# Products before a norm finished by halves of the rows, in a two-block float32 kernel

## The chip, the core and the metric

The kernel runs on one core of a Trainium2 chip. The metric is the device time of one execution in microseconds; the kernel before takes 1652.35 us (median of 3 runs, 1651.98 to 1653.06). A core has a matrix engine (TensorE, PE in the profile), a vector engine (VectorE, DVE), an activation engine (ScalarE, ACT), GpSimd (POOL) and a queue for transfers (SyncE, SP). Each works through its own list of instructions in order; semaphores connect them.

## The reference

Two transformer-like blocks, one after the other, on 512 rows (528 with 16 meta rows in the first block) of 1024 channels, in float32. What matters here is the shape that both have:

```python
h_res = h_res + rmsnorm(merged @ w_out, g_mix_post)          # out1, norm post1
h2 = rmsnorm(h_res, g_ffn_pre)                               # norm pre1f
up = centred_dwconv(h2 @ w_up, conv_w_ffn, conv_b_ffn)       # up1: 2 x 2816 channels
a, v = jnp.split(up, 2, axis=-1)
ffn_out = (jax.nn.gelu(a) * v) @ w_down                      # down1
h_res = h_res + rmsnorm(ffn_out, g_ffn_post)                 # norm post1f
```

`rmsnorm(x, g)` divides every row by the root of its mean square over the channels (plus 1e-6) and multiplies by the gain. The second block begins with another such norm (`pre2`) and a large product (first its gated part, `glu`, then the attention heads), and ends in the same way: `out2`, norm `post2`, norm `pre2f`, `up2`, `down2`, norm `post2f`.

## The kernel before

Channels lie on the 128 partitions, rows along the free dimension: the residual `res` is 8 channel blocks of 128 partitions by 528 rows. A product is made tile by tile, a tile being 128 output channels of all rows. The weights stream through four slots in pieces of 128 x 1024 numbers: SP loads a piece into `raw` as soon as the piece four before it is used (`w_used`), ScalarE writes its upper part (`w_to_hi`, L774) and VectorE the rest (`w_to_lo`, L1088). Operands are split in the same way, and a product is three passes (upper by upper, upper by rest, rest by upper; `three_passes`, L464). A one-piece tile is 8 channel steps k of three passes, in 512 columns or two times 258. A tile of `down` needs three pieces, 22 steps.

A norm of the output of a product goes as follows. ScalarE squares each finished tile (L782) and writes it, times the gain, into `mix1`, `mix2` or `down` (L939, L867, L1054); VectorE adds the squares up in `acc` (L1099). After the last tile TensorE sums over channels with a matmul by ones (`sum_channels`, L551), ScalarE takes the root (L788), VectorE inverts it (`inverse`, L1106 to L1110), and TensorE spreads the inverse over the partitions (`spread_inverse`, L562). `to_residual` (L1134) then does, for each of 8 blocks, a product (L1146 or L1148), an addition to `res` (L1150) and the rest part of the next operand (`cut_lo`, L1116), whose upper part ScalarE makes (L818 in `cut_residual`).

The norm in front of the next product isn't applied to its operand: the product begins on the unscaled residual, and each tile is scaled afterwards. So `norm_tiles` (L484) computes tiles 0 to 2 block by block as the operand appears, while ScalarE squares the residual and VectorE adds (`inverse_of_res`, L1129); then it sums the channels, and spreads the inverse in the middle of tile 3. ScalarE copies it into `rstd` (L798, L796), and from there on VectorE scales tile after tile, convolves, multiplies (`two_pairs`, per two pieces), and splits the weights in between, in a written order. ScalarE's order after the squares is: root, load of the table for the next function, upper part of piece 4, `rstd`, upper parts of pieces 5 and 6.

After `post2f` there is no next product: VectorE multiplies 8 blocks (L1620), GpSimd adds three of them to `res` (L451), VectorE five (L1623), and SP stores them.

## Time and profile before

| | us |
|---|---|
| median of 3 runs | 1652.35 |
| profiled execution, its own time | 1651.44 |
| its span, first to last instruction | 1649.6 |
| TensorE busy (matmuls) | 1590.9 |
| VectorE busy | 1108.0 |
| ScalarE busy | 549.6 |
| weight pieces, 272 of 512 KB | landing 3.5 each (median) |

The span counts from the first to the last instruction; the engines overlap, so their busy times don't add up to it. A busy time is a sum of instructions; consecutive matmuls overlap too, so a single one's duration is longer than its share, and the time of many divided by their number is what one costs.

### The profile page before, as it was taken

Reading aid. Unit: us, or ns where it says so; the run is one execution under the profiler, and the core shown is the slowest. Engines: PE = TensorE matmul, PEld = TensorE weight load, DVE = VectorE, ACT = ScalarE, POOL = GpSimd, SP = SyncE. Lnnn points to the kernel's source line nnn. Section 1 sums busy time; section 2 is a strip of 40 time slices with the busy share of each in tenths; the row PEclk is TensorE's granted clock in tenths of the full one; section 3 lists DMA queues with packets and bytes.
Section 4 is the critical chain, followed back from the end, with each engine's and each line's share of the span. In section 5 each row is a group of like instructions: output and inputs, shape, how many; then the busy total and the mean of one; then the engine's idle time right before and its main releaser. Section 6 shows DMA issues by size and latency. Waiting matters only on the chain.

```text
span 1649.6 us, 24134 instructions
## 1 busy us (share of the span) xinstructions
PE 1590.9 (96%) x9246; PEld 1408.3 (85%) x9246; DVE 1108.0 (67%) x1544; ACT 549.6 (33%) x742; POOL 34.3 (2%) x65
## 2 busy tenths in 40 slices
PE   8999999899999999989999999999998999999996
PEld 8999999899999988868887878877786788887885
DVE  5334456589888842277899998875556899887223
ACT  5123323342222232243333333556233322222231
POOL 1110000000000000000001001000000000000000
PEclk9999999899999999989999999999998999999998
DMA  4443212222323333323332222222322323332332
GB/s 168 122 122 96 93 52 90 64 90 90 89 89 91 96 95 114 102 70 93 98 90 83 77 84 84 80 75 82 97 90 63 100 92 102 91 100 89 113 104 76
DMA packets 43904, 152.51 MB, mean 92 GB/s; under 512 B 5850, under 2 KB 5862, under 8 KB 43840
## 3 DMA queue, kind: packets, MB, share of 16 engines
q1 hardware_dynamic: 41760, 147.26, 28.7%
q0 software_dynamic: 2080, 4.34, 1.1%
q8 instruction: 46, 0.75, 0.2%
q14 instruction: 18, 0.15, 0.0%
HBM read 149.44 MB, written 4.51 MB: 93 GB/s over the span
## 4 chain that ended last, share of the span: by engine, by line
PE 80%; DVE 14%; ACT 3%; DMA 1%; issue 1%; POOL 0%; DVEq 0%; SPq 0%; ACTq 0%
PE ps L464 77%; DVE work L1406 6%; DVE wlo L1088 2%; ACT whi L774 1%; DVE res L1150 1%; PE ps L562 1%; PE ps L651 1%; DVE tmp L1146 1%; PE ps L724 1%; DMA stats_dram<-head_stats 1%; DVE acc L1129 1%; ACT probs L973 0%; DMA raw<-w_dram 0%; DVE peaks L1450 0%; ACT L1019 0%
## 5 line engine op out<-in xcount | busy, mean ns | idle before, releaser
L464 PE MATMUL ps<-xh,whi 128*128 128x258 f32 (+2 forms) x2048 | 579.6, 331 | 16.2 <-DVE wlo L1088 8.9
L464 PE MATMUL ps<-xh,wlo 128*128 128x258 f32 (+2 forms) x2048 | 572.2, 328 | 0.0
L464 PE MATMUL ps<-xl,whi 128*128 128x258 f32 (+2 forms) x2048 | 571.8, 328 | 0.0
L1088 DVE TENSOR_TENSOR wlo<-raw,whi 128x1024 fp32r<-128x1024 f32 x272 | 331.9, 1220 | 167.2 <-ACT whi L774 166.6
L774 ACT ACTIVATE whi<-raw 128x1024 fp32r<-128x1024 f32 x272 | 287.0, 1058 | 438.4 <-DMA raw<-w_dram 438.2
L464 PEld LDWEIGHTS ps<-xh,whi 128*128 128x128 f32 x2048 | 347.8, 191 | 49.8 <-issue 17.2
L464 PEld LDWEIGHTS ps<-xh,wlo 128*128 128x128 f32 x2048 | 346.6, 190 | 33.8
L464 PEld LDWEIGHTS ps<-xl,whi 128*128 128x128 f32 x2048 | 347.2, 190 | 31.6 <-issue 0.5
L1406 DVE SCALAR_TENSOR_TENSOR work<-cin,vecs,work 128x512 f32<-128x512 f32 x240 | 180.2, 751 | 6.8
L464 PE MATMUL ps<-fh,whi 128*128 128x512 f32 x352 | 137.1, 390 | 2.3 <-DVE stage L1163 1.2
L464 PE MATMUL ps<-fl,whi 128*128 128x512 f32 x352 | 137.0, 389 | 0.0
L464 PE MATMUL ps<-fh,wlo 128*128 128x512 f32 x352 | 137.0, 389 | 0.0
L1099 DVE TENSOR_TENSOR acc<-acc,sq 128x512 f32<-128x512 f32 (+1 forms) x40 | 27.7, 693 | 121.4 <-ACT sq L782 121.3
L1163 DVE TENSOR_TENSOR stage<-ps,rstd 128x516 f32<-128x516 f32 x57 | 39.6, 695 | 68.1 <-PE ps L464 65.8
L464 PEld LDWEIGHTS ps<-fh,whi 128*128 128x128 f32 x352 | 66.1, 188 | 16.7 <-DVE stage L1158 1.6
L464 PEld LDWEIGHTS ps<-fl,whi 128*128 128x128 f32 x352 | 66.1, 188 | 13.7
L464 PEld LDWEIGHTS ps<-fh,wlo 128*128 128x128 f32 x352 | 66.1, 188 | 13.6
L1170 DVE SCALAR_TENSOR_TENSOR work<-stage,vecs,work 128x512 f32<-128x512 f32 x88 | 66.1, 752 | 10.6 <-DVE work L1167 1.5
L1167 DVE SCALAR_TENSOR_TENSOR work<-stage,vecs,work 128x512 f32<-128x512 f32 x88 | 66.2, 752 | 10.6 <-DVE work L1202 1.5
L782 ACT ACTIVATE sq<-ps 128x512 f32<-128x512 f32 (+1 forms) x32 | 19.2, 599 | 141.1 <-PE ps L464 141.1
L847 ACT ACTIVATE work<-work 128x512 f32<-128x512 f32 x44 | 27.8, 632 | 89.6 <-DVE work L1170 89.5
L464 PE MATMUL ps<-x2h,whi 128*128 128x512 f32 x128 | 51.0, 399 | 3.6 <-DVE x2l L1116 3.6
(201 smaller groups left out, 1510.9 us busy)
## 6 DMA issues: line engine op xcount, KB each, us to landing
raw<-w_dram SPq DMA_DIRECT2D x272, 512.0 KB, 3.5
bias_copies_dram<-bias_rows_dram POOLq DMA_DIRECT2D x12, 192.0 KB, 3.8
res<-x_dram SPq DMA_DIRECT2D x8, 264.0 KB, 6.1
out_dram<-res SPq DMA_DIRECT2D x8, 256.0 KB, 2.1
dftp<-dftp_dram POOLq DMA_DIRECT2D x1, 550.7 KB, 4.6
bias<-bias_copies_dram POOLq DMA_DIRECT2D x4, 128.0 KB, 2.3
bias<-bias_copies_dram POOLq DMA_DIRECT2D x8, 64.0 KB, 2.5
vecs<-vec_dram SPq DMA_DIRECT2D x1, 364.0 KB, 8.2
```

Source lines behind the costliest of these rows:

```text
L464: last = pe.matmul(ps[:, bank, 0:b - a], w[:, slot, cols], xx[:, k, a:b], start=start and n == 0, stop=stop and n == 2)
L562: last = pe.matmul(ps[:, bank, at_:at_ + w], inv[0:w, part, b:b + 1].broadcast_to([w, P]), ident_r[0:w, 0:w], start=(part == 0), stop=(par ...
L651: last = pe.matmul(ps[:, 2 * (g % 2) + part, 0:HALF1], pa[0:ROWS, g % 2, r, part * P:(part + 1) * P], dftp[0:ROWS, r, part, :], start=(r = ...
L774: act.activation(whi[:, slot, :], raw[:, slot, :], ACT.Copy).then_inc(w_hi, 1)
L782: act.activation(dst, src, ACT.Square).then_inc(sq_ready, 1)
L847: act.activation(work[:, 1, 0:SEQ], work[:, 0, 0:SEQ], ACT.Gelu_apprx_tanh) \
L1088: dve.tensor_tensor(wlo[:, slot, :], raw[:, slot, :], whi[:, slot, :].bitcast(F32), ALU.subtract).then_inc(w_split, 1)
L1099: dve.tensor_tensor(acc[:, 0:width], acc[:, 0:width], sq[:, slot, 0:width], ALU.add) \
L1163: dve.tensor_tensor(halves(dst), tile_psum(slot, True), halves(by), ALU.mult).then_inc(tile_read, 1)
L1167: step(dve.scalar_tensor_tensor(out=dst, in0=src(at_, width), scalar=vec(w, tile), in1=dst, op0=ALU.mult, op1=ALU.add))
L1170: last(dve.scalar_tensor_tensor(out=dst, in0=src(at_ + 2, width), scalar=vec(w, tile + 2 * tiles), in1=dst, op0=ALU.mult, op1=ALU.add))
L1406: ins = dve.scalar_tensor_tensor(out=dst, in0=src, scalar=vec("conv_dw_w_2", t * KD + m), in1=dst, op0=ALU.mult, op1=ALU.add)
```

## The change

The last tiles of each product before a norm (tiles 4 to 7 of `out`, 6 and 7 of `down`) are computed in two rounds: first all of them for the first half of the rows, then all for the second half (`halved_tiles`). The weights of the tiles of both rounds stay in the four slots. In the second round TensorE sums the channels of the first half at its step 4 and spreads their inverse at its step 8. VectorE updates the residual for the first half of the rows (8 blocks) and then for the second half (`update_by_halves`), with the additions of the second round's squares and the splits of the next product's pieces 0 to 3 at written places between them; ScalarE does likewise (`cut_by_halves`). The next product computes tiles 0 and 1 for the first half, interleaved, with the second half's sum after k = 4; then the second half's spread, tile 2 for the first half, and tiles 0 to 2 for the second half (`norm_tiles_by_halves`). The sum of the norm in front of the product now follows tile 3, and its spread stands in the middle of tile 4. The two tiles that `down` and `out2` halve, and tiles 0 to 2 of `glu` and `up2`, are two passes of 256 columns instead of one of 512. At the end VectorE applies the first half's update (8 products and 8 additions of 256 columns) beside the second round, and only the second half behind it; the output leaves in 16 stores instead of 8. `x2h`, `x2l` and others get other places in memory; `x2h` lies on the first blocks of `down1`'s operand. `half_passes` is `three_passes` for one half; `add_half`, `updated` are the half-row forms of L1099 and of L1146 with L1150. In `squares_of_res` ScalarE reads tile 0 of `up1` out (`unscaled`) after the third square; before, it did so after the eighth.

```diff
+HALF_TILES = {"post1": (4, 5, 6, 7), "post1f": (6, 7), "post2": (4, 5, 6, 7), "post2f": (6, 7)}
+HALF_AT = {"post1": 0, "post1f": 4, "post2": 6, "post2f": 10}
+FIRST_HALF_AFTER = {4: {-1: 0, 1: 1, 3: 2, 5: 3}, 2: {-1: 0, 5: 1}}
...
-PAIRS_OF = {"u": (0, 3, 1, 0), "up1": (0, 3, 1, 0, 3, 1, 0, 2, 3, 1, 0, 1),
-            "glu": (0, 1, 2, 3, 5, 6, 7, 3), "up2": (0, 1, 2, 3, 5, 6, 7, 3)}
+PAIRS_OF = {"u": (0, 3, 1, 0), "up1": (0, 3, 1, 0, 3, 1, 2, 0, 3, 1, 0, 1),
+            "glu": (0, 1, 2, 3, 5, 6, 7, 4), "up2": (0, 1, 2, 3, 5, 6, 7, 4)}
+KEPT = {"up1": 2, "glu": 3, "up2": 5}
...
+        x2h = put("x2h", [P, KD, SEQ], F32R, offset=big)
+        x2l = put("x2l", [P, KD, SEQ], F32R, offset=big + KFF * SEQ * 4)
...
+            def halved_tiles(phase, norm, steps, operand, spans, banks, free):
+                for h in range(2):
+                    at = 0
+                    for n, kts, k0, t, first, final in steps:
+                        if h == 0:
+                            pe.wait_ge(w_split, C0[phase] + n + 1)
+                        if (h, t) in free:
+                            pe.wait_ge(*free[h, t])
+                        for k in range(kts):
+                            if h == 1 and at == 4:
+                                sum_channels(norm, 0)
+                            if h == 1 and at == 8:
+                                spread_inverse(norm, 0)
+                            last = half_passes(banks[h][t], 0, n % 4, k, k0 + k, operand, spans[h],
+                                               first and k == 0, final and k == kts - 1)
+                            at += 1
+                        if h == 1:
+                            last.then_inc(w_used, 1)
+                        elif final:
+                            last.then_inc(half_done, 1)
+            def norm_tiles_by_halves(phase, operand, spans, ready, post, pre, row):
+                pairs = PAIRS_OF[phase]
+                def three(p, k, h):
+                    bank, at_ = (2 * pairs[p] + h, 0) if phase == "up1" else (pairs[p], h * SEQ // 2)
+                    return half_passes(bank, at_, p, k, k, operand, spans[h], k == 0, k == KD - 1)
+                for k in range(KD):
+                    for p in (0, 1):
+                        if k == 0:
+                            pe.wait_ge(w_split, C0[phase] + p + 1)
+                            if p == 0:
+                                pe.wait_ge(half_read, HALF_AT[post] + len(HALF_TILES[post]))
+                            else:
+                                pe.wait_ge(tile_read, T0[phase] - 1)
+                        if p == 0:
+                            pe.wait_ge(operand_ready, ready + k + 1)
+                        three(p, k, 0)
+                    if k == 4:
+                        sum_channels(post, 1)
+                spread_inverse(post, 1)
+                pe.wait_ge(w_split, C0[phase] + 3)
+                for k in range(KD):
+                    three(2, k, 0)
+                pe.wait_ge(tile_read, T0[phase])
+                for k in range(KD):
+                    pe.wait_ge(operand_ready, ready + KD + k + 1)
+                    for p in range(3):
+                        last = three(p, k, 1)
+                        if k == KD - 1:
+                            last.then_inc(w_used, 1)
+                for n in range(3, len(pairs)):
+                    before = [m for m in range(n) if pairs[m] == pairs[n]]
+                    if n == (6 if phase == "up1" else 7):
+                        pe.wait_ge(rstd_ready, KEPT[phase])
+                    one_piece_tile(phase, n, n % 4, pairs[n], before[-1] + 1 if before else 0, operand, row,
+                                   (lambda: spread_inverse(pre)) if n == 4 else None)
+                    if n == 3:
+                        sum_channels(pre)
...
+            def down_tiles(dn, post, f_name):
+                half2 = [(0, SEQ // 2), (SEQ // 2, SEQ)]
+                banks = ((2, 6), (3, 7))
+                pe.wait_ge(tile_read, T0[dn])
...
+                pe.wait_ge(tile_read, T0[dn] + 4)
+                for c in range(2):
+                    pe.wait_ge(w_split, C0[dn] + 18 + c + 1)
+                    for k in range(KD):
+                        for h in range(2):
+                            last = half_passes(banks[h][0], 0, (18 + c) % 4, k, KD * c + k, (fh, fl), half2[h],
+                                               c == 0 and k == 0, False)
+                    last.then_inc(w_used, 1)
+                steps = [(20, 6, 2 * KD, 0, False, True), (21, KD, 0, 1, True, False), (22, KD, KD, 1, False, False),
+                         (23, 6, 2 * KD, 1, False, True)]
+                halved_tiles(dn, post, steps, (fh, fl), half2, banks, {})
...
+            def half_tile(post, t, h, bank, dst, gain):
+                tiles = HALF_TILES[post]
+                i = tiles.index(t)
+                n = SQ[post] + tiles[0] + len(tiles) * h + i
+                w, blocks = NORMS[post]
+                if h == 0:
+                    act.wait_ge(half_done, HALF_AT[post] + i + 1)
+                square(n, ps[:, bank, 0:w * blocks], sq[:, n % 2, 0:w * blocks])
+                act.activation(dst[:, t, h * w * blocks:(h + 1) * w * blocks], ps[:, bank, 0:w * blocks], ACT.Identity,
+                               scale=vec(gain, t)).then_inc(tile_read if h else half_read, 1)
+            def cut_by_halves(post, pre, phase, func, gain, a, second_half, dst):
+                w = NORMS[post][0] * NORMS[post][1]
+                after = FIRST_HALF_AFTER[len(HALF_TILES[post])]
+                root(post, 0)
+                for h in range(2):
+                    for k in range(-1, KD):
+                        if k >= 0:
+                            if k == 0 and h == 0 and pre == "pre2":
+                                act.wait_ge(w_used, C0["down1"] + 22)
+                            act.wait_ge(res_ready, UPDATE_AT[post] + KD * h + k + 1)
+                            act.activation(dst(k)[:, h * w:(h + 1) * w], res[:, k, a + h * w:a + (h + 1) * w],
+                                           ACT.Identity, scale=vec(gain, k)).then_inc(x_hi, 1)
+                        if h == 0 and k in after:
+                            second_half(after[k])
+                        if h == 0 and k in (2, 4, 6):
+                            w_to_hi(phase, 0, k // 2 - 1)
+                    if h == 0:
+                        root(post, 1)
+                        w_to_hi(phase, 0, 3)
+                squares_of_res(pre, phase, a, a + 2 * w)
+                after_squares(pre, phase, func)
...
+            def update_by_halves(post, pre, phase, src, a, gain, hi_part, lo_part):
+                w = NORMS[post][0] * NORMS[post][1]
+                after = FIRST_HALF_AFTER[len(HALF_TILES[post])]
+                def lower(k, h):
+                    c0, c1 = h * w, (h + 1) * w
+                    cut_lo(CUT_AT[pre] + KD * h + k + 1, k, gain, a + c0, a + c1, hi_part(k)[:, c0:c1],
+                           lo_part(k)[:, c0:c1])
+                inverse(post, 0)
+                for h in range(2):
+                    if h == 0:
+                        add_half(post, after[-1], 1)
+                    dve.wait_ge(spread_ready, NTH[post, h])
+                    for k in range(KD):
+                        updated(post, k, h, src, a)
+                        if k:
+                            lower(k - 1, h)
+                        if h == 0 and k in after:
+                            add_half(post, after[k], 1)
+                        if h == 0 and k in (3, 5):
+                            w_to_lo(phase, 0, (k - 3) // 2)
+                        if h == 1 and k == 3:
+                            w_to_lo(phase, 0, 3)
+                    lower(KD - 1, h)
+                    if h == 0:
+                        inverse(post, 1)
+                        w_to_lo(phase, 0, 2)
...
-            inverse("post2f")
-            dve.wait_ge(spread_ready, NTH["post2f"])
+            inverse("post2f", 0)
+            add_half("post2f", 0, 1)
+            dve.wait_ge(spread_ready, NTH["post2f", 0])
             for k in range(KD):
-                dve.tensor_tensor(down[:, k, :], down[:, k, :], ps[:, STAT, :], ALU.mult).then_inc(update_ready, 1)
+                updated("post2f", k, 0, down, N_META)
+                if k == 5:
+                    add_half("post2f", 1, 1)
+            inverse("post2f", 1)
+            dve.wait_ge(spread_ready, NTH["post2f", 1])
+            c0 = SEQ // 2
+            for k in range(KD):
+                dve.tensor_tensor(down[:, k, c0:SEQ], down[:, k, c0:SEQ], stat("post2f", 1), ALU.mult) \
+                   .then_inc(update_ready, 1)
             for k in range(TAIL_POOL, KD):
                 dve.wait_ge(update_ready, k + 1)
-                dve.tensor_tensor(res[:, k, N_META:L1], res[:, k, N_META:L1], down[:, k, :], ALU.add) \
-                   .then_inc(res_ready, 1)
+                cols = res[:, k, N_META + c0:L1]
+                dve.tensor_tensor(cols, cols, down[:, k, c0:SEQ], ALU.add).then_inc(res_ready, 1)
```

## Rows read from the trace of the kernel before

**Rows 1.** Busy time in the four stretches between products (from : to, length, engines, clock).
```profile
312.00:322.20 10.20, 3.67 (x24) 3.46 (x25) 7.07 (x12) 4.89 (x7) 0.00 (x0) 0.71 0.14 51
701.70:711.30 9.60, 3.06 (x17) 2.81 (x17) 7.08 (x12) 4.88 (x7) 0.00 (x0) 0.69 0.17 55
1257.70:1267.30 9.60, 3.05 (x17) 2.81 (x17) 7.02 (x12) 4.88 (x7) 0.00 (x0) 0.71 0.18 55
1633.70:1649.60 15.90, 2.95 (x16) 2.68 (x16) 9.08 (x17) 1.44 (x3) 3.72 (x3) 0.61 0.35 132
```
**Rows 2.** Instructions in order of time after out1: start, duration, engine, line.
```profile
311.56 0.40 PE L464 MATMUL ps<-mgh,wlo 128*128 128x258 f32 x2
...
313.54 1.08 PE L551 MATMUL ps<-ones,acc 128*86 128x1 f32 x12 [1.59 <-DVE acc L1099]
...
316.01 2.59 PE L562 MATMUL ps<-ident_r,inv 86*128 86x86 f32 x12 [1.38 <-DVE inv L1110]
...
318.64 0.69 DVE L1148 TENSOR_TENSOR tmp<-mix,ps 128x516 f32<-128x516 f32 x1 [0.59 <-PE ps L562]
...
322.20 0.77 PE L464 MATMUL ps<-xh,whi 128*128 128x258 f32 x2 [3.60 <-DVE xl L1116]
```
**Rows 3.** Busy time by stretch again; the clock is the third number from the end.
```profile
316.30:326.50 10.20, 6.59 (x32) 6.47 (x32) 8.95 (x13) 3.38 (x5) 0.00 (x0) 0.50 0.01 2
...
879.30:882.20 2.90, 0.02 (x1) 0.00 (x0) 1.52 (x3) 2.90 (x8) 1.31 (x2) 1.00 0.50 153
882.85:886.25 3.40, 3.40 (x10) 2.62 (x9) 3.29 (x6) 0.68 (x1) 1.11 (x2) 0.50 0.01 0
```
**Rows 4.** VectorE in order of time, one channel block of the update.
```profile
329.97 0.68 DVE L1148 TENSOR_TENSOR tmp<-mix,ps 128x516 f32<-128x516 f32 x1
...
331.30 0.75 DVE L1116 SCALAR_TENSOR_TENSOR xl<-res,vecs,xh 128x516 fp32r<-128x516 f32 x1
331.97 0.69 DVE L1148 TENSOR_TENSOR tmp<-mix,ps 128x516 f32<-128x516 f32 x1
```
**Rows 5.** In order of time, the norm before up1.
```profile
336.70 4.70 DVE L1129 TENSOR_TENSOR acc<-acc,sq 128x516 f32<-128x516 f32 x6 [0.70 <-ACT sq L824]
...
344.14 1.06 ACT L774 ACTIVATE whi<-raw 128x1024 fp32r<-128x1024 f32 x1
...
346.85 0.60 ACT L798 ACTIVATE rstd<-ps 128x516 f32<-128x516 f32 x1 [1.65 <-PE ps L562]
...
365.64 1.22 DVE L1088 TENSOR_TENSOR wlo<-raw,whi 128x1024 fp32r<-128x1024 f32 x1
```
**Rows 6.** In order of time: rstd and the split of piece 7, glu and up2.
```profile
735.20 0.60 ACT L796 ACTIVATE rstd<-ps 128x512 f32<-128x512 f32 x1 [1.08 <-PE ps L562]
...
747.80 1.22 DVE L1088 TENSOR_TENSOR wlo<-raw,whi 128x1024 fp32r<-128x1024 f32 x1
...
1291.15 0.60 ACT L796 ACTIVATE rstd<-ps 128x512 f32<-128x512 f32 x1 [1.06 <-PE ps L562]
...
1309.65 1.22 DVE L1088 TENSOR_TENSOR wlo<-raw,whi 128x1024 fp32r<-128x1024 f32 x1
```
**Rows 7.** Groups of one shape: count, busy time, mean ns of one.
```profile
L1323 DVE TENSOR_TENSOR work<-tmp,ps 128x253 f32<-128x253 f32 x4 | 1.7, 420 | 8.4 <-ACT tmp L922 8.4
```
**Rows 8.** The chain that ended last: start, duration, what.
```profile
265.53 46.44 PE ps L464 x384
...
341.66 0.87 PE ps L551 x12
...
345.54 1.27 PE ps L562 x12
...
581.73 119.96 PE ps L464 x528
```
**Rows 9.** In order of time, the products of the tail.
```profile
1639.04 4.87 DVE L1620 TENSOR_TENSOR down<-down,ps 128x512 f32<-128x512 f32 x8 [1.99 <-PE ps L562]
```
**Rows 10.** Transfers of the page: count, size, us from issue to landing.
```profile
raw<-w_dram SPq DMA_DIRECT2D x272, 512.0 KB, 3.5
```

401 lines of the change are left out of this document (217 added, 184 removed).

## The prediction

> **What bounds the kernel now.** I read the page's busy times, then the stretches between two products, then the order of time inside one of them. The page shows TensorE at work nearly all the time, so what can be won is the four places where it stands still: after `out1`, `down1`, `out2`, `down2`. There it is empty for 10.2, 9.6, 9.6 and 15.9 us, with only 3 to 4 us of tiny matmuls and a granted clock of about 0.7 on average [rows 1]. Inside the first one the reader sees one serial chain: last matmul ending at 311.96, channel sums, root and inverse, spread, then VectorE's first update at 318.64 and the first matmul of `up1` at 322.20 [rows 2]. The clock is at its half level, 1.2 GHz, from 316.3 to 326.5 [rows 3], so the first 4 us of `up1` also run at half pace, worth 2 us. The change attacks about 12 us in each of three places.
>
> But those stretches hold a second chain, VectorE's, and it goes on after TensorE has restarted. VectorE updates eight channel blocks at 2.00 us each, 329.97 to 331.97 [rows 4], adds eight squares until A = 341.40, lets TensorE spread the next norm, and first has the scale R = 347.45 (ScalarE's copy) [rows 5]. Then it needs 19.4 us until it has split weight piece 7 at 366.87 [rows 5]. TensorE can use that piece at about 367.0 (tiles 4 to 6 follow the spread without a gap), so the margin is 0.1 us. In `up2` the same split, 1309.65 + 1.22, is what TensorE waits for [rows 6]. Around `up1` and `up2`, then, the time is set by R, not by when the first tile starts. That is my main choice.
>
> **What one half costs.** A whole two-input pass is 0.69 us [rows 4]; 253 columns take 0.420 [rows 7], so 258 or 256 take about 0.425: half the columns cost 62%, not 50%. The pass with a scalar (0.75) should take 0.485 by the same difference. A block's cycle goes from 2.00 to 1.195 us per half, 2.39 for both: eight blocks cost 19.1 instead of 16.0. Bounds: 1.0 (exactly half) to 1.3 per half. The Trainium skill, "VectorE: DVE Perf Modes", the TRN2 errata section, says a large tile pays the fixed latency once and many small ones pay it each time, which speaks against this change; its table's 58 + columns cycles would give 0.33 us for 256 columns, and 3 us less per boundary, but our 253-column row is 0.420 and decides.
> On TensorE 384 matmuls of 258 columns take 46.44 us (0.121 each), 528 of 512 take 119.96 (0.227 each) [rows 8]. Where tiles were already in two spans (`out1`, `up1`) halves are free; a 512-column pass becomes 2 x 0.1195, +0.012: 96 passes of `out2` +1.2 us, 132 of each `down` +1.6 us. Each first-half sum and spread, once in the gap, is now in line: half of 0.87 and half of 1.27 [rows 8], about 1.0 us.
>
> **After out1.** Let z be the end of the last tile's first half. Before, E (last matmul) = z+11.5, A = z+41.0, R = z+47.0.
> First half: from the sums' start to the spread's 2.5 us passed before [rows 2]; with three blocks about 2, so the spread asked for at k-step 8 (z+3.35) just doesn't wait. Tile 4's second-half square must be added first; VectorE starts at z+4.4. Eight cycles 9.6, last lower part 0.5, three more adds 1.05, two weight splits (pieces 0, 1, after k=3 and 5) 2.3: z+17.9. Waits: 1.1 for tile 5's second half (TensorE at z+6.9), then twice 0.8 and once 0.4 because ScalarE converts a piece (1.06) and a block ahead of the square. It ends at z+21.0.
> TensorE ends the product at z+12.7 and stalls. `norm_tiles_by_halves` interleaves tiles 0 and 1, its first step of tile 1 needs piece 1, which VectorE splits at z+17.7. That is 4.4 us idle, and everything behind it on the queue waits, `sum_channels(post, 1)` after k=4 too (z+21.0). Root and inverse, three more k-steps, spread: VectorE's second half starts at z+24.3. 9.6 + 0.5 + one split 1.15 give z+35.5.
> Squares of the residual as before, plus one `unscaled` put between (0.5): A' = z+42.6, 1.7 later than before, though the update began 14 us earlier.
> Then the moved spread. Before it sat in the middle of tile 3, whose weights were there: A to R 6.05 us. Now it sits in the middle of tile 4, and piece 4 is converted only behind the root and a table load: from A to ScalarE's conversion at 344.14 (sums, root, table) 2.74, high part 1.06, low part 1.22 [rows 5], handovers 0.1: 5.1; half a tile 2.9, spread 1.27, copy 0.65: 9.95. R' = z+52.6, +5.6; piece 7 at R'+19.4 against 367.0: **+5.4 us**. Tiles 0 to 3 are hidden meanwhile.
>
> **After out2.** Same walk with four blocks: E is 2.2 earlier against z than E' = z+12.4; R = z+44.3 [rows 6]. Half tiles are a little shorter (0.25) and no `unscaled` is put in: A' = z+41.9, R' = A' + 9.35 = z+51.3. **+7.0 us**.
>
> **After down1.** E' = z+11.0, E = z+8.4. VectorE runs freer (two halved tiles, two adds), but ScalarE's first cut waits for piece 21 (z+6.0), because x2h lies on f's memory. First half done z+19.0 (TensorE again waits for piece 1, 4.3 us), second half z+22.1 to 33.2, A' = z+39.8, R' = z+49.2 against z+42.5. `glu` asks less of VectorE: piece 7 is split 13.2 us after R (735.80 to 749.02) [rows 6], so at z+62.4; TensorE wanted tile 7 at z+60.8 before. **+1.6 us**.
>
> **Tail.** Nothing of a next product is behind it. The eight products (4.87 us [rows 9], 0.61 each) become half passes of 0.35, 2.8; five adds at the same pitch, 3.1, become 1.8; VectorE still ends blocks 6 and 7 of the first half before the inverse (0.7). From the last matmul 11.3 us instead of 15.9, less 2.6 for halves and sum in line: **-2.0 us**.
>
> Weight pieces 4 to 7 (20 to 23) must lie in all four slots for the first halves. Piece 7 has 8.7 us from its slot being free; landing 3.5 [rows 10], high, low and a square before them make 6.8. I put it at nothing; with landings of 6 us it would cost 1.
>
> **Clock.** An idle stretch of 2.9 us (879.3 to 882.2) was followed by 3.4 us at clock 0.50 [rows 3]. The change makes two stretches of over 4 us in each of three places: waiting for piece 1 and, after tile 3, for piece 4. Both are followed by TensorE work that VectorE waits for. A 3.4 us dip costs 0 (inside the idle time) to 1.7 each; I take 0.85: six make **+5.1 us**. The Trainium skill ("TensorE: Matmul & The Clock Gate", what's actually happening) says that the throttled state is the default and activity releases it; the rows agree. A gate that ignored idle time would give 0 here, the sum 12.
>
> Sum: 5.4 + 7.0 + 1.6 - 2.0 + 5.1 = +17.1 on a profiled span of 1649.6, which is 1.84 under its own time 1651.44, itself 0.9 under the median of 1652.35. So 1652.35 + 17.1, **1669.5 us**.
>
> **Rivals.**
> 1. The gap is really covered, *faster*: TensorE works from E' on. Then 10.2, 9.6 and 9.6 us of gap and three times 2 of slow clock go, 35.4, less 1.0, 2.6 and 2.2 of costs in line, and 2 more in the tail: about -31, 1621. For it: 12 us of TensorE work lie beside the first half's update. Against it: it decides whether VectorE is through with the first half's eight blocks within some 6 us of E'; I get 8.3, with piece 1 behind block 5. If it is met only partly (R no later than before), the result is some 5 to 10 us faster. 0.16.
> 2. The halves cost half (cycle 1.0, 3 us less per boundary) and no dip follows: +12 - 9 = +3, and with ScalarE's waits gone nothing measurable. Against it the 0.420 row. 0.12.
> 3. The clock falls for as long as it did before, about 10 us, at each of the three places: the k-loop before `sum_channels(post, 1)` runs wholly at half pace, 2.5 us more each beyond my 0.85, and again for part of tile 4. +27 to +30, 1681. For it: the average in the gaps was 0.7; against it: TensorE was empty longer then. 0.12.
> That the halves don't overlap at all (VectorE starting only at E') I exclude by the queue order.
>
> **How the numbers follow.** My case has 0.60, own range 1661 to 1675. Under 1650 lies nearly all of rival 1, above 1681 half of rival 3; that leaves out 2 in 10, so 1650 to 1681. A measurement of this kernel tells about 0.2%, 3.3 us: faster 0.17 (rival 1 and a shade), same 0.09 (most of rival 2), slower 0.74.
>
> **What would show it.** Idle time of TensorE ended by VectorE's weight split, over 3 us, right after each product; a second one before the product tile that holds the spread; block cycles of about 1.2 us on VectorE; ScalarE's `rstd` copy 5 to 10 us later, counted from the first halves' end; in `up1` a wait for the split of piece 7; a tail of about 11 us. I am wrong if the first `rstd` copy isn't later, or if TensorE is busy from product to product.

## The result, and the profile after

The changed kernel takes 1674.57 us (median of 4 runs, 1673.81 to 1676.95) against 1652.43 for the kernel before on the same chip (1651.98 to 1653.06): ratio 1.0134, 95% interval 1.0122 to 1.0146. That is 22.1 us slower, where +17.1 was predicted; it lies in the range and at the upper edge of my own one (1661 to 1675). The page of the changed kernel begins so (engine, busy us, instructions):

```profile
span 1673.0 us, 25145 instructions
PE 1604.2 (96%) x9750; PEld 1440.0 (86%) x9750; DVE 1122.0 (67%) x1656; ACT 559.5 (33%) x794; POOL 32.7 (2%) x65
```

TensorE is busy for the same share of a longer span. Its instructions in order of time behind `out1` answer to [rows 2]:

```profile
312.90 0.29 PE L496 MATMUL ps<-xh,wlo 128*128 128x258 f32 x1
317.11 0.58 PE L496 MATMUL ps<-xh,whi 128*128 128x258 f32 x1 [3.93 <-DVE wlo L1266]
...
322.76 0.55 PE L687 MATMUL ps<-ones,acc 128*86 128x1 f32 x6
325.41 0.76 PE L699 MATMUL ps<-ident_r,inv 86*128 86x86 f32 x6
...
339.88 0.47 PE L486 MATMUL ps<-xh,whi 128*128 128x258 f32 x2 [0.83 <-ACT stage L925]
...
345.72 1.01 PE L687 MATMUL ps<-ones,acc 128*86 128x1 f32 x12
350.71 0.80 PE L486 MATMUL ps<-xh,whi 128*128 128x258 f32 x2 [3.98 <-DVE wlo L1266]
...
356.03 1.65 PE L699 MATMUL ps<-ident_r,inv 86*128 86x86 f32 x12
...
363.13 0.66 PE L486 MATMUL ps<-xh,whi 128*128 128x258 f32 x2 [2.49 <-DVE wlo L1266]
...
377.77 0.50 PE L486 MATMUL ps<-xh,whi 128*128 128x258 f32 x2 [1.34 <-DVE wlo L1266]
```

The gap of 10.2 us is gone, and four waits for a weight split have come: piece 1 (3.93), piece 4 (3.98), piece 5 (2.49), piece 7 (1.34). VectorE runs ahead with the first half, as meant, and TensorE finds the next weights missing. At 345.72 stand the sums of the norm in front of `up1`, 1.5 us behind the end of VectorE's adds (344.19). Before, the two met, the adds ending at 341.40:

```profile
341.50 1.03 PE L551 MATMUL ps<-ones,acc 128*86 128x1 f32 x12
```

ScalarE over the second norm, the answer to [rows 5]:

```profile
346.77 0.26 ACT L908 ACTIVATE roots<-ps,small 86x6 f32<-86x6 f32 x1 [2.53 <-PE ps L687]
347.05 1.28 ACT L943 ACT_TABLE_LOAD   x1
348.34 1.06 ACT L894 ACTIVATE whi<-raw 128x1024 fp32r<-128x1024 f32 x1
357.72 0.60 ACT L918 ACTIVATE rstd<-ps 128x516 f32<-128x516 f32 x1 [8.33 <-PE ps L699]
```

`rstd` is copied at 357.72, against 346.85 before: from the conversion of piece 4 ScalarE waits 8.33 us for TensorE's spread, before 1.65. Stretches at half clock, the answer to [rows 3] (the clock is the third number from the end):

```profile
315.60:322.40 6.80, 5.29 (x24) 5.29 (x25) 4.26 (x9) 2.08 (x4) 0.00 (x0) 0.50 0.03 12
349.60:356.40 6.80, 5.69 (x27) 5.70 (x27) 1.05 (x1) 0.00 (x0) 0.00 (x0) 0.50 0.00 0
363.20:366.60 3.40, 3.40 (x16) 3.40 (x17) 3.16 (x6) 0.00 (x0) 0.00 (x0) 0.52 0.15 57
718.20:725.00 6.80, 6.05 (x29) 6.05 (x29) 3.48 (x8) 1.85 (x3) 0.00 (x0) 0.51 0.01 4
749.00:755.80 6.80, 4.58 (x11) 3.61 (x12) 1.48 (x2) 0.91 (x1) 0.00 (x0) 0.50 0.06 26
1281.40:1284.80 3.40, 3.40 (x18) 3.40 (x18) 2.12 (x6) 1.85 (x3) 0.00 (x0) 0.51 0.02 5
1312.30:1315.70 3.40, 3.40 (x9) 2.63 (x9) 0.00 (x0) 0.00 (x0) 0.00 (x0) 0.51 0.00 0
1322.40:1325.80 3.40, 3.26 (x8) 2.58 (x9) 3.16 (x6) 0.00 (x0) 0.00 (x0) 0.51 0.19 75
```

Before there was one such stretch per place, of 10.2 us. The two that the rows ahead don't show:

```profile
705.50:715.70 10.20, 6.41 (x19) 5.31 (x20) 9.21 (x14) 3.77 (x5) 0.00 (x0) 0.50 0.00 0
1261.80:1272.00 10.20, 6.56 (x19) 5.40 (x20) 9.28 (x14) 3.60 (x5) 0.00 (x0) 0.50 0.00 0
```

In the three together TensorE was busy for 19.6 of 30.6 us. Now there are two or three per place, of 3.4 or 6.8 us, and it was busy for 35.1 of 40.8. As half of the busy time at half clock is lost, that is an estimated 17.5 us lost against 9.8, and part of it falls on work that VectorE waits for. VectorE, one block of the second half ([rows 4] before), and the tail:

```profile
333.71 0.48 DVE L1304 SCALAR_TENSOR_TENSOR xl<-res,vecs,xh 128x258 fp32r<-128x258 f32 x1
334.11 0.42 DVE L1329 TENSOR_TENSOR tmp<-mix,ps 128x258 f32<-128x258 f32 x1
334.57 0.43 DVE L1332 TENSOR_TENSOR res<-res,tmp 128x258 f32<-128x258 f32 x1
334.91 0.48 DVE L1304 SCALAR_TENSOR_TENSOR xl<-res,vecs,xh 128x258 fp32r<-128x258 f32 x1
...
1665.75 2.73 DVE L1833 TENSOR_TENSOR down<-down,ps 128x256 f32<-128x256 f32 x8 [0.75 <-PE ps L699]
```

A block's cycle is 1.20 us per half (333.71 to 334.91), 2.40 for both against 2.00. Where the 23.4 us of span went, by the first matmul of each stage (worked out from rows of both traces):

```
                        before    after   difference   predicted (clock included)
out1 -> down1           316.20   327.07     +10.9         5.4 + 1.7
down1 -> pw             587.73   593.91      +6.2         1.6 + 1.7
pw -> down2             344.25   353.33      +9.1         7.0 + 1.7
down2 -> end            135.89   133.57      -2.3        -2.0
```

(`pw` is the product ahead of `out2`. The four differences add up to 23.8; `out1` itself began 0.4 us sooner, at 265.12 against 265.53. The second line holds the attention as well, which by itself moves by 1 us and more between profiled runs of one code.)

### The profile page after: what moved, and what is told of

Its sections match the earlier page's. It is cut to its first block, busy times and chain, and to the rows that moved or that the text cites. A ratio compares the mean times of both kernels' runs of the same rounds, so it can differ in the third digit from the quotient of the medians.

```text
span 1673.0 us, 25145 instructions
## 1 busy us (share of the span) xinstructions
PE 1604.2 (96%) x9750; PEld 1440.0 (86%) x9750; DVE 1122.0 (67%) x1656; ACT 559.5 (33%) x794; POOL 32.7 (2%) x65
## 4 chain that ended last, share of the span: by engine, by line
PE 80%; DVE 13%; ACT 4%; DMA 1%; issue 1%; POOL 0%; SPq 0%; DVEq 0%
PE ps L486 69%; PE ps L496 8%; DVE work L1612 5%; DVE wlo L1266 3%; ACT whi L894 1%; DVE res L1332 1%; PE ps L777 1%; DVE tmp L1329 1%; PE ps L699 1%; DMA stats_dram<-head_stats 1%; ACT probs L1152 0%; PE ps L846 0%; DVE peaks L1656 0%; PE ps L687 0%; DMA head_stats<-stats_dram 0%
## 5 line engine op out<-in xcount | busy, mean ns | idle before, releaser
L486 PE MATMUL ps<-xh,whi 128*128 128x258 f32 (+2 forms) x1944 | 548.7, 331 | 25.1 <-DVE wlo L1266 22.4
L486 PE MATMUL ps<-xh,wlo 128*128 128x258 f32 (+2 forms) x1944 | 541.2, 327 | 0.0
L486 PE MATMUL ps<-xl,whi 128*128 128x258 f32 (+2 forms) x1944 | 541.0, 327 | 0.0
L486 PEld LDWEIGHTS ps<-xh,whi 128*128 128x128 f32 x1944 | 330.3, 191 | 56.9 <-DVE wlo L1266 15.3
L486 PEld LDWEIGHTS ps<-xh,wlo 128*128 128x128 f32 x1944 | 329.2, 190 | 31.6
L486 PE MATMUL ps<-fh,whi 128*128 128x512 f32 x264 | 102.9, 390 | 1.6 <-DVE stage L1373 0.8
L486 PE MATMUL ps<-fl,whi 128*128 128x512 f32 x264 | 102.7, 389 | 0.0
L486 PE MATMUL ps<-fh,wlo 128*128 128x512 f32 x264 | 102.7, 389 | 0.0
L1277 DVE TENSOR_TENSOR acc<-acc,sq 128x512 f32<-128x512 f32 (+1 forms) x28 | 19.4, 692 | 70.0 <-ACT sq L902 66.4
L902 ACT ACTIVATE sq<-ps 128x512 f32<-128x512 f32 (+3 forms) x44 | 21.1, 480 | 125.4 <-PE ps L486 84.1
L486 PEld LDWEIGHTS ps<-fl,whi 128*128 128x128 f32 x264 | 49.6, 188 | 10.2
L486 PEld LDWEIGHTS ps<-fh,wlo 128*128 128x128 f32 x264 | 49.6, 188 | 10.2
L496 PE MATMUL ps<-xh,whi 128*128 128x256 f32 (+1 forms) x160 | 48.6, 303 | 9.2 <-DVE wlo L1266 7.8
```

The source lines that it names most:

```text
L486: last = pe.matmul(ps[:, bank, 0:b - a], w[:, slot, cols], xx[:, k, a:b], start=start and n == 0, stop=stop and n == 2)
L496: last = pe.matmul(ps[:, bank, at_:at_ + b - a], w[:, slot, cols], xx[:, k, a:b], start=start and n == 0, stop=stop and n == 2)
L902: act.activation(dst, src, ACT.Square).then_inc(sq_ready, 1)
L1277: dve.tensor_tensor(acc[:, 0:width], acc[:, 0:width], sq[:, slot, 0:width], ALU.add) \
```

## The experiments

Two theories stood against each other. Mine: the time of `up1` and `up2` hangs on the moment at which `rstd` is there, and the change delays it. The rival: it hangs on TensorE's restart, and what was lost is the clock. A third question was whether halves could pay once repaired. Every run had the kernel before beside it on its chip; where two kernels of different chips are compared below, it is by their distances from that one: +22.1 us for the changed kernel. The intervals put some 2 to 3 us of uncertainty on each distance, and about 3 on the difference of two, so small gains are read from the traces.

**e1: sum before tile 3, spread inside tile 3.** In `norm_tiles_by_halves`, whose weights for tile 3 are there:

```diff
+                sum_channels(pre)
                 for n in range(3, len(pairs)):
...
-                                   (lambda: spread_inverse(pre)) if n == 4 else None)
-                    if n == 3:
-                        sum_channels(pre)
+                                   (lambda: spread_inverse(pre)) if n == 3 else None)
```

> The changed kernel with one part undone: the sum of the norm before a product stands ahead of tile 3 again and its spread in the middle of tile 3, as before the change. Theory (the time of the rstd copy decides; the spread in tile 4 waits for the split of piece 4): in the changed kernel A' to R' takes 14.1 us (344.2 to 358.3), here sum 0.9, half of tile 3 at a slow clock 5.3, spread and copy 2.3: 8.5, so R' is 5.6 us earlier after out1 and out2, some 3 after down1: 1660 us (1657 to 1664). Rival (the cost is the doubled number of smaller instructions and passes, the order does nothing): unchanged, 1674.6. A second rival (TensorE's idle time before tile 3, now some 5 us, costs as much as it saves): 1671 or more.

Measured: 1668.24 us, ratio 1.0101 (1.0084 to 1.0118). `rstd` came 5.7 us sooner from the start of `out1` (86.9 against 92.6), the waits for pieces 5 and 7 went, and `down1` 5.6 us sooner. But TensorE, ahead of VectorE's adds, now stood idle before the sums:

```profile
344.19 1.92 PE L686 MATMUL ps<-ones,acc 128*86 128x1 f32 x12 [5.18 <-DVE acc L1316]
```

and the stretch at half clock, which began within that wait (341.5), was 10.2 us long. At the other two places `rstd` gained 3.5 and 2.3 us only, and the stage behind `down1` became longer (below). Against the kernel before on its own chip it is +16.8 us, 5.3 less than the changed kernel's 22.1: under half of what was expected (14.6).

**e2: tile 0 of the first half alone**, so that piece 1 is wanted 3 us later:

```diff
...
                 for k in range(KD):
...
+                    pe.wait_ge(operand_ready, ready + k + 1)
+                    three(0, k, 0)
+                    if k == 4:
+                        sum_channels(post, 1)
+                pe.wait_ge(w_split, C0[phase] + 2)
...
+                for k in range(KD):
+                    three(1, k, 0)
+                    if k == 1:
+                        spread_inverse(post, 1)
```

> The changed kernel, but TensorE computes tile 0 for the first half alone, with the second half's sum after its k = 4, and only then tile 1, with the spread after its k = 1, so that the sum no longer waits for the split of piece 1. Theory (that wait is on the path of VectorE's second half): the second half starts at about z+22.2 instead of z+26.2, z being the end of the first halves, so each of three places gets 4 us earlier: 1662.5 us (1660 to 1666). Rival (VectorE's own work sets the pace, the idle TensorE costs nothing): within 2 us of 1674.6.

Measured: 1670.87 us, ratio 1.0116 (1.0099 to 1.0133), +19.4 against before, a gain of 2.7, which is within the uncertainty and far from the expected 12. The 3.9 us wait became four of 0.41 to 1.71, and the clock fell all the same:

```profile
319.30:329.50 10.20, 10.20 (x51) 10.09 (x52) 7.92 (x19) 3.21 (x7) 0.00 (x0) 0.55 0.01 2
```

`rstd` at the first place moved by 0.15 us (92.45): the expected gain is missing there, and the waits for pieces 4, 5 and 7 are as they were. What was gained lies behind `down1`.

**e3: both.**

> Both edits of the two runs before in one kernel: tile 0 first, spread in tile 3. Theory: the gains add, since they lie one behind the other on the same chain up to the rstd copy (4 us before A', 5.6 behind it): 1650 us (1646 to 1655), level with the kernel before the change or just under it. Rival (one hides the other): as the better of the two, 1660 or more.

Measured: 1658.59 us, ratio 1.0044 (1.0027 to 1.0061), +7.1 against before: a gain of 15.0 us, more than the 5.3 and 2.7 of its parts. That fits with each part alone having moved TensorE's waiting to another place. It is still slower than before, and 1650 was expected.

**e4: the waits of the changed kernel filled** with 30 matmuls of no use before piece 1 and 30 before piece 4, order unchanged.

> The changed kernel with 30 matmuls of 224 columns (about 3.2 us at full clock), whose result nobody reads, in each of the two idle stretches of TensorE at each of three places: ahead of the first step of tile 1, and behind the sum that follows tile 3. No wait is removed. Theory (the clock falls in the two idle stretches, and the matmuls behind them, run at the half level, are on the path): the first dip costs 1.9 us and the second about 3 at each place, so about 12 to 14 us go: 1662 (1658 to 1667). With the size that I took in the prediction, 0.85 for each of six, 1669.5. Rival (the slow clock lies beside waits and costs nothing): 1674.6, or up to 2 more if the added matmuls come in the way.

Measured: 1664.97 us, ratio 1.0082 (1.0065 to 1.0099), +13.5 against before, a gain of 8.6. The first 30:

```profile
313.97 3.50 PE L565 MATMUL ps<-xh,ident_r 128*128 128x224 f32 x30
```

The half-clock stretches behind both waits are gone at all three places, `rstd` is 4.8 us sooner at the first (87.78), and the waits for pieces 5 (2.49) and 7 (2.58) stay. So the clock behind the two waits was about 8.6 us of the 22.1 (with some 3 of uncertainty), near the expected 12 to 14 but short of it; of the rest, the stretches behind piece 5 are still clock, and what remains isn't.

**e5: only the tail by halves**, `out1`, `down1` and `out2` in the old form (the order of the buffers and the places in memory stay those of the changed kernel):

```diff
+HALVED = ('post2f',)
...
+                if post not in HALVED:
+                    one_piece_tiles(phase, KD, operand, row, ready)
+                    sum_channels(post)
+                    spread_inverse(post)
+                    return
```

> The kernel before, with only the last product (down2) finished by halves; the three products that another product follows end as before. Theory (each place is priced by itself, the tail gains 2.3 us there): 1652.4 - 2.3 = 1650 us, -0.14%, at the edge of what can be told. Rival (what the tail gained in the change came out of something earlier in the program, down2 starting in another state): 1652.4 or above. The stretch from TensorE's last matmul to the end should be 11 us instead of 15.9.

Measured: 1651.02 us, ratio 0.9994 (0.9985 to 1.0003). `down2` to the end is 133.55 us as in the changed kernel (135.89 before), so the tail's 2.3 us are there in the trace; the times can't tell the whole from no change.

**e6 and e8: e5 with the old gaps filled**, 12 + 12 + 30 matmuls of 128 columns, then 10 + 10 + 24 of 256 (before the sums, before the spread, behind it):

```diff
                     one_piece_tiles(phase, KD, operand, row, ready)
+                    keep_busy(12)
                     sum_channels(post)
+                    keep_busy(12)
                     spread_inverse(post)
+                    keep_busy(30)
```

> As e5, and in the three other gaps, which are as in the kernel before, TensorE gets small matmuls of no use (12 of 128 columns before the channel sums, 12 before the spread, 30 after it), so that it is busy while it waits. Theory (two chains tied: VectorE's chain to weight piece 7 sets the time of up1 and up2, TensorE's restart that of glu): the clock stays high, TensorE does the first tiles some 2 us sooner, but piece 7 comes only 0.5 us sooner, by the first spread at full clock; so 0.5 to 0.6 us each around up1 and up2 and about 2 around glu: 1650 - 3 = 1647 us, with a wait for a weight split late in up1 and up2. Rival (TensorE's restart alone sets the time): 3 us at each place, 1641 us. Second rival (the half clock after a gap was no cost): 1650 us, as e5, or slightly more.

> As e6, but the useless matmuls are 256 columns wide instead of 128 (10 before the channel sums, 10 before the spread, 24 behind it). In e6 the clock fell although TensorE was busy: it was at half level for 13.7, 13.7 and 10.2 us, and rstd came 2.5 us later than in e5 at the first place, as did down1. Theory (the width of the matmuls holds the clock, as the 224-column ones did in e4, and rstd alone sets the time of up1 and up2): the spread runs at full clock, rstd some 1 us sooner than in e5 (R - start of out1 80.4 against 81.44), but TensorE's own margin is small, so 0 to 1 us at each place: 1648 to 1651 us. Rival (the width is not it): as e6, 1654 us. Second rival (TensorE's restart sets the time): 1642 us.

Measured: 1653.94 (ratio 1.0012, 1.0003 to 1.0021) and 1655.52 us (1.0018, 1.0009 to 1.0027). Both missed: 1647 and 1648 to 1651 were expected. Of e6, the stretch at half clock behind `out1`:

```profile
314.90:328.50 13.60, 13.60 (x65) 13.54 (x65) 11.70 (x19) 4.68 (x6) 0.00 (x0) 0.50 0.01 1
```

TensorE was busy for all of it, and the clock was at half. The useless matmuls at half clock then delayed the spread (`rstd` 2.5 us later than in e5) and `down1` by the same 2.5. In e8 TensorE comes through the gap sooner, so at the second and third places it stood idle before the second sums instead (2.53 and 2.56 us), and 6.8 us of half clock began there. At the third it ran to the spread:

```profile
1289.79 1.77 PE L757 MATMUL ps<-ones,acc 128*128 128x1 f32 x8 [2.56 <-DVE acc L1401]
1296.69 1.04 PE L769 MATMUL ps<-ident_r,inv 128*128 128x128 f32 x8
```

```profile
1289.90:1296.70 6.80, 6.80 (x21) 5.64 (x22) 1.74 (x4) 2.60 (x3) 0.00 (x0) 0.50 0.28 99
```

**e7: e3 with its waits filled**, by 14 matmuls of 128 columns behind the sums of the second half, and 20 (`glu`) or 30 before the sums of the next norm.

> The changed kernel with both reorderings of e3 (sum of the next norm before tile 3 and its spread inside that tile, tile 0 of the first half alone) and matmuls of no use where TensorE would stand idle (14 after the sum of the second half, 20 to 30 before the sum of the next norm). Theory (what is left of the loss in e3, 1658.6, is mostly the half clock around the second norm): 1658.6 - 3 x 2 = 1652 to 1653 us, so halving with every repair gives back nothing but its own tail. Rival (the clock was all that was wrong with it): 1640 to 1645, below e6. Second rival (the filling delays the sums it stands before): 1658 or more.

Measured: 1659.7 us, ratio 1.0045 (1.0031 to 1.0058), no better than e3; 1652 to 1653 was expected, and the second rival said 1658 or more. In this trace the clock still fell, for 6.8 to 10.2 us behind the sums of the second half and at two places for 3.4 us around the next sums.

**e9: halves without overlap.** As e5, with each update pass as two passes over half the columns:

```diff
-                            step(dve.tensor_tensor(row, src[:, k, :], stat(post), ALU.mult))
...
+                        for h in range(2):
...
+                            step(dve.tensor_tensor(row[:, h * c:(h + 1) * c], src[:, k, h * c:(h + 1) * c], by, ALU.mult))
```

> As e5 (only the tail by halves), but in the three other places VectorE does each of its three update passes of a channel block as two passes over half the columns, with nothing overlapped and TensorE as before. This prices the halves alone. Theory (a half costs 62% and rstd sets the time): the block cycle goes from 2.00 to 2.4 us, rstd comes 3.1 us later at each place, and all of it is seen in the time of up1 and up2, less around glu: 1651 + 3.1 + 3.1 + 2 = 1659 us. Rival (halves cost half, or the chain over rstd has slack): 1651 us.

Measured: 1660.38 us, ratio 1.0047 (1.0034 to 1.006), +8.8 against before, where e5 was -0.9: 9.6 us more, as expected (1659). VectorE in order of time:

```profile
319.53 0.75 DVE L1435 TENSOR_TENSOR tmp<-mix,ps 128x258 f32<-128x258 f32 x2
320.31 0.77 DVE L1439 TENSOR_TENSOR res<-res,tmp 128x258 f32<-128x258 f32 x2
320.99 0.88 DVE L1416 SCALAR_TENSOR_TENSOR xl<-res,vecs,xh 128x258 fp32r<-128x258 f32 x2
321.79 0.75 DVE L1435 TENSOR_TENSOR tmp<-mix,ps 128x258 f32<-128x258 f32 x2
```

The cycle is 2.26 us, not 2.4: two halves back to back cost less than two that wait for one another (2.40 in the changed kernel). 8 x 0.26 is 2.1 us of VectorE at each place; `rstd` came 2.2, 1.9 and 3.5 us later.

**e10: squares early**, to take VectorE's waits for ScalarE (0.36 and 0.70 us before the adds) out of e5:

```diff
                         act.activation(dst(k), res[:, k, a:a + w], ACT.Identity, scale=vec(gain, k)).then_inc(x_hi, 1)
+                        if k in (4, 5):
+                            act.activation(sq[:, k % 2, 0:w], res[:, k - 4, a:a + w], ACT.Square) \
+                               .then_inc(sqp_ready, 1)
...
+                        if k == KD - 1:
+                            dve.tensor_tensor(acc[:, 0:w], sq[:, 0, 0:w], sq[:, 1, 0:w], ALU.add) \
+                               .then_inc(sqp_used, 2)
```

> As e5, but ScalarE squares the first two updated blocks during the update, and VectorE adds them ahead of the last lower part, so that VectorE doesn't wait for ScalarE between update and sums (0.36 and 0.70 us of waits in the kernel before). Theory (two chains are tied within 0.1 us): rstd comes 1.0 us sooner and the time changes by 0.1 to 0.3 us at each place: 1650.5 us. Rival (rstd alone sets it, TensorE has slack): -1 us at each place, 1648 us.

Measured: 1648.66 us, ratio 0.9979 (0.997 to 0.9988). The theory said 1650.5 and the rival 1648, so the time alone speaks for the rival; the trace of the first place speaks for the theory. There the adds end 74.0 us after the start of `out1`, in e5 76.0: of the 2.0, 1.1 are the waits, and 0.7 is that the update began sooner, because more of the first spread ran before the clock fell. But TensorE isn't yet at the sums, and `rstd` gains 0.26 us against e5. `glu` is 1.9 us shorter than in e5's profiled run, which had one stretch at half clock more there. In order of time (VectorE's adds end at 340.71, the sums begin at 342.62):

```profile
336.01 4.70 DVE L1393 TENSOR_TENSOR acc<-acc,sq 128x516 f32<-128x516 f32 x6
...
342.62 1.01 PE L746 MATMUL ps<-ones,acc 128*86 128x1 f32 x12
...
343.96 0.19 DVE L1370 RECIPROCAL roots<-roots 86x6 f32<-86x6 f32 x1 [3.26 <-ACT roots L967]
```

**e11: e8 and e10 together.**

> e8 and e10 together: both chains shorter. Theory: TensorE starts up1, glu and up2 some 3 us sooner in work done, rstd comes 2 us sooner, so 2 us at each place: 1651 - 6 = 1645 us, below all kernels so far. Rival (filling doesn't hold the clock): as e10 or e6, 1650 or more. Second rival (some third thing binds at these places, a transfer or the splits of pieces 5 to 7): 1649.

Measured: 1647.56 us, ratio 0.9971 (0.996 to 0.9982). Behind `out1` the clock held (the stretch of [rows 1]), and both chains are shorter (ScalarE, from a start of `out1` at 265.50; the window and the `rstd` copy):

```profile
312.00:322.20 10.20, 8.69 (x74) 8.11 (x73) 7.68 (x13) 4.87 (x7) 0.00 (x0) 1.00 0.19 53
```

```profile
344.75 0.60 ACT L988 ACTIVATE rstd<-ps 128x516 f32<-128x516 f32 x1 [1.62 <-PE ps L769]
```

It is 2.6 us above the expected 1645: behind `down1` and `out2`, 3.4 us of half clock fell at the second sums (from about 728.6 and 1285.0), and `rstd` there is no sooner than in e10. The intervals of e10 and e11 overlap.

**e12: e11 filled only behind out1.**

> e11 with its useless matmuls kept only behind out1. In the profiled runs of e10 and e11, filling behind out1 brought rstd 1.93 us sooner (81.18 to 79.25 from the start of out1) and down1 1.93 us sooner; behind down1 and out2 it brought rstd 0.4 and 0.8 us later (153.37 to 153.73, 121.13 to 121.94), where the half clock falls into the wait before the second sums instead. Theory (the time of each place is rstd plus a constant, 234.85 us to down1 and 222.2 to down2): out1 to down1 314.1, out2 to down2 343.3, in all 1 us less than e11: 1646.6 us. Rival (the places are not independent, what is gained at the first is lost behind it): 1648.7, as e10.

Measured: 1648.86 us, ratio 0.9979 (0.9969 to 0.9989), on a chip where the kernel before took 1652.58; 1646.6 was expected, and the rival said 1648.7. In the profiled run, which at 1647.15 us is the fastest of the nine, `out1` to `down1` is 314.25 and `pw` to `down2` 343.37, as expected; the stretch between them is as long as in e11 and e10 (588.6), so the whole can't be told from either.

**What all of them say together.** R is the start of the `rstd` copy, counted like the stage from its first matmul (us, of the profiled runs):

```
                  out1 place: R  to down1  rest  |  out2 place: R  to down2  rest
before                    81.32   316.20  234.88 |          121.69   344.25  222.56
changed                   92.60   327.07  234.47 |          131.17   353.33  222.16
e1                        86.94   321.43  234.49 |          128.83   351.00  222.17
e2                        92.45   326.92  234.47 |          131.32   353.49  222.17
e3                        86.51   320.99  234.48 |          125.28   347.46  222.18
e4                        87.78   323.78  236.00 |          128.09   350.27  222.18
e5                        81.44   316.29  234.85 |          121.70   343.87  222.17
e6                        83.96   318.81  234.85 |          122.46   344.63  222.17
e7                        85.76   320.25  234.49 |          123.45   345.63  222.18
e8                        80.79   315.64  234.85 |          124.90   347.08  222.18
e9                        83.65   318.13  234.48 |          125.18   347.34  222.16
e10                       81.18   316.03  234.85 |          121.13   343.30  222.17
e11                       79.25   314.10  234.85 |          121.94   344.11  222.17
e12                       79.41   314.25  234.84 |          121.20   343.37  222.17
```

R varies by 13 us, the rest by 0.4 (but for e4, where a half-clock stretch of 3.4 us fell behind piece 7). At these two places whatever moved R moved the time by as much, in both directions. That alone doesn't tell R from TensorE's own progress, for behind the spread of the kernel before TensorE waits for nothing in `up1`. What tells them apart is the place of the spread. In the changed kernel, e2 and e4 it stands one tile (5.8 us of `up1`) later than in the others, so TensorE has a tile less left to do; the rest is the same, because TensorE then waits for pieces 5 and 7.

Behind `down1` it is otherwise ("attention" is the first matmul of the product for the heads, counted like R from the first matmul of `down1`):

```
            down1 place: R   to attention    rest   spread in tile
before              153.47         221.36   67.89         3
changed             165.06         228.06   63.00         4
e1                  161.55         229.44   67.89         3
e2                  162.26         225.26   63.00         4
e3                  155.59         223.48   67.89         3
e4                  160.22         223.19   62.97         4
e5                  155.00         222.90   67.90         3
e10                 153.37         220.98   67.61         3
```

(The rest of e6 to e9, e11 and e12, all with the spread in tile 3, is 67.87 to 67.90.)

With the spread a tile later the rest is 4.9 us shorter, and e1, whose R came 3.5 us sooner than the changed kernel's, took 1.4 us longer. Where the spread stands in tile 3, the split of piece 7 is done some 5 us before TensorE comes to it (749.02 and 754.1 in the kernel before), TensorE waits for nothing behind the spread, and R is no more than a mark on TensorE's own way: what it lost before decides. In the changed kernel the two chains meet within 0.1 us (split done at 771.06, tile 7 begun at 771.17). What TensorE waited for there ahead of R:

```profile
718.95 0.58 PE L496 MATMUL ps<-x2h,whi 128*128 128x256 f32 x1 [3.81 <-DVE wlo L1266]
...
746.30 0.95 PE L687 MATMUL ps<-ones,acc 128*128 128x1 f32 x8
751.22 0.79 PE L486 MATMUL ps<-x2h,whi 128*128 128x512 f32 x1 [3.98 <-DVE wlo L1266]
```

## Why the prediction was right, and where its sizes were not

- **What sets the time: right for `up1` and `up2`.** "The time is set by R, not by when the first tile starts" holds there in the kernels above, but for e4's late stretch. It is also why a gap of 10 us that vanishes brought nothing. Before, TensorE reached the second sums behind `out1` at 341.50, just as VectorE's adds had ended (341.40). After, the adds ended later against z, and TensorE had spent the time won at the restart on waits of 3.93, 0.72 and 0.83 us and on the half clock: it reached the sums at 345.72, 1.5 us behind the adds. "Tiles 0 to 3 are hidden meanwhile" was wrong by that.
- **Two chains within 0.1 us: right in kind.** e10 took 1.1 us of waits out of VectorE's chain alone and got 0.26 of R at the first place, because the sums then waited for TensorE. e11, with TensorE sooner as well, got 2.1 against before.
- **The cost of halves: right.** 1.195 us per half block was predicted, 1.20 measured. From [rows 7] came 0.425 us for 258 columns and 0.485 with a scalar; the rows show 0.42 to 0.43, and 0.48. Half cost (rival 2) is out. By e9 the halves alone, with nothing overlapped, cost 9.6 us in all, though its cycle is 2.26 us.
- **First half and the wait for piece 1: right.** VectorE was done at z+20.3 (21.0 predicted, z = 299.98); TensorE waited 3.93, 3.81 and 3.90 us (4.4 and 4.3 predicted).
- **The moved spread: right in kind, too small.** A' to R' was put at 9.95 us and took 14.1 (344.19 to 358.32). Of the 4.2 missing, 1.5 is that the sums stood behind tile 3, which had itself waited 0.83 us for ScalarE's read of a buffer (the row at 339.88), and most of the rest is half clock: half of tile 4 took 5.3 us, not 2.9, and the spread 1.65, not 1.27. A' itself was 1.6 late (z+44.2), because the k-steps ahead of the second half's spread ran at half clock (second half at z+26.2, not 24.3).
- **The clock: the term that was mis-sized.** I gave each of six stretches 0.85 us, 5.1 in all, taking 3.4 us for its length from [rows 3] and half of it as hidden. Four of the six were 6.8 us, and a further one of 3.4 came behind piece 5 at two places. e4, which removes those behind the two waits, prices them at 8.6 us. With 8.6 in the place of 5.1 the sum is +20.6, of 22.1 measured; e4 leaves a new stretch of its own, so 8.6 is rather low, and it is known to some 3 us only. The windows agree with its size: by their estimate TensorE lost 7.7 us more at half clock than before, not all of it on the path.
- **After down1: low, because R' was.** +6.2 measured against 3.3; `glu` alone, `down1` to the attention, went from 221.36 to 228.06 us, +6.7. With z = 703.65 there, VectorE's adds ended at z+42.2 (39.8 predicted) and A' to R' took 12.0 us (9.4): R' = z+54.2, 5.0 late. The split of piece 7 followed it by the predicted 13.2 us, so that the 1.6 becomes 6.6. Most of what came behind A' is the half clock again: half of tile 4 took 5.0 us (751.22 to 756.21), not 2.7. Counted along TensorE it comes out alike: its waits are 8.5 us (3.81, 0.68, 3.98) where they were 7.1, an estimated 5.3 us were lost at half clock where it was 3.2 (half of the busy time in the windows above), and the remaining 3.2 is work. The profiled run of e5 took 222.90 us with the old form of this stage, because a further stretch at half clock fell there (731.4 to 734.8); so a stage can move by 1.5 us from run to run for that reason alone.
- **The tail: right**, -2.3 against -2.0, in every kernel that had it (133.5 to 134.0 us).
- **Rival 1** (the gap covered) failed where the prediction put it: VectorE wasn't through the first half by the product's end. But e3 shows that mere order, with the waits and clock falls that came of it, cost 15 of the 22 us. **Rival 3** (long clock fall, +27 to +30) was nearer to the truth than its 0.12 suggests: stretches of 6.8 us fell where it put them, though not of 10.

What is left of halving when its order is repaired: e3 against e5 is +8.0 us (7.1 and 0.9), where the passes by halves alone cost 9.6 (e9 against e5). The overlap thus gave some 2 us back, which is no more than the uncertainty of such a difference, not the 12 per place that the gaps seemed to offer.

## What to carry to other kernels

Before covering an idle gap, find what the time behind it hangs on, and how much later that comes if each pass is cut in two; here the distance from the stage's start to `rstd`, plus a constant, gives the time of both `up` stages to 0.4 us in all kernels but e4. Ask it for each place: behind `down1` it doesn't, because TensorE's own waits decided in most kernels. Moving the spread by one tile tells which it is: where what is left behind it shrinks, TensorE's own way decides. When work is moved ahead, check that each thing it then needs (here weight pieces split by the very engine that is now busier) comes sooner too. Where two chains are tied, shorten both or gain little: with the tail by halves in both, early squares and filled gaps were 0.29% faster than the kernel before (e11), early squares without filling 0.21% (e10), which can't be told apart.

## What the hardware did that I had not expected

- **A busy TensorE can be at half clock.** In e6 it was busy for 13.6 of 13.6 us at clock 0.50 (128-column matmuls around the sums). With 256 columns the clock fell at the first place for 6.8 us in the profiled run of e8 and not at all in those of e11 and e12, whose gap code is the same. What decides between these the runs do not show. The Trainium skill ("TensorE: Matmul & The Clock Gate", what's actually happening) says that activity releases the throttled state; e4 agrees (no half clock behind the filled waits), e6 does not, if busy time is taken for activity.
- **Half-clock stretches came in lengths of 3.4, 6.8, 10.2 and 13.7 us**, around waits of 1 to 5 us. The length doesn't follow from the wait: in the changed kernel the waits for piece 1 were 3.93, 3.81 and 3.90 us, and the stretches behind them 6.8, 6.8 and 3.4.
- **Removing one wait creates another, with its clock fall.** e1 and e8 moved TensorE's idle time to the next place at which it met VectorE, the second sums (5.18 us, and 2.53 and 2.56), and e2 broke one wait into four with 10.2 us of half clock around them. Each lost a part or all of the gain.
